# ScalarE instead of SyncE begins the stores of the expert output rows

## The reference, cut to what matters

```python
ids = g_top[:, None] * EXPERTS_PER_GROUP + e_idx          # two experts for each token
gates = jnp.einsum('nk,nke->ne', g_w * e_w, jax.nn.one_hot(ids, N_EXPERTS))
for e in range(N_EXPERTS):
    a = jax.nn.silu(hf @ w_e_gate[e]) * (hf @ w_e_up[e])  # 1024 -> 512, twice
    out = out + gates[:, e:e + 1] * (a @ w_e_down[e])     # 512 -> 1024
```

## Time and profile before

| | |
|---|---|
| runs | 1700.65, 1700.78, 1700.83 us |
| profiled execution | span 1698.5 us from first to last instruction; with the 2.3 us around it, the 1700.8 us of the runs |
| TensorE, VectorE, ScalarE busy | 1633.7, 1331.4, 1035.4 us |
| experts | about 340 to 912 us |
| stores of expert rows | 35 on SyncE's queue: 10 of 512 KB, 8 of 256 KB, 17 of 128 KB |

### The profile page before, as it was taken

The page is one execution under the profiler, slowest core; times in us unless marked ns, Lnnn a source line. Parts: engine busy times, 40 slices in busy tenths (PEclk is TensorE's granted clock), DMA queues, the critical chain, the costliest instruction groups (busy, mean ns, idle before and its releaser), DMA issues.

```text
span 1698.5 us, 27843 instructions
## 1 busy us (share of the span) xinstructions
PE 1633.7 (96%) x10558; PEld 1427.5 (84%) x10558; DVE 1331.4 (78%) x1522; ACT 1035.4 (61%) x1145; POOL 64.0 (4%) x58
## 2 busy tenths in 40 slices
PE   8999989999999999999998998999999999999998
PEld 7998879878877677777776987999999999998887
DVE  6546897874589999999996897778767979777776
ACT  4333676554678999999987554554444484453443
POOL 0000000000000000000003340000000020000000
PEclk9999999999999999999999999999999999999999
DMA  9663126085789999999999443446555455445550
GB/s 327 191 191 103 54 72 202 9 322 184 269 342 422 422 422 423 422 423 423 423 420 338 144 164 105 149 149 202 195 176 171 152 191 185 144 141 194 195 175 25
DMA packets 186669, 393.26 MB, mean 232 GB/s; under 512 B 6992, under 2 KB 151120, under 8 KB 162000
## 3 DMA queue, kind: packets, MB, share of 16 engines
q1 hardware_dynamic: 184496, 383.89, 61.8%
q0 software_dynamic: 2080, 8.10, 1.3%
HBM read 381.34 MB, written 10.62 MB: 231 GB/s over the span
## 4 chain that ended last, share of the span: by engine, by line
PE 58%; DMA 16%; DVE 14%; issue 6%; ACT 5%; SPq 0%; POOL 0%; DVEq 0%; ACTq 0%; POOLq 0%
DMA raw<-w_e_up_dram 13%; PE ps L979 9%; DVE wlo L2377 7%; PE ps L693 5%; PE ps L698 5%; PE ps L985 5%; PE ps L694 5%; PE ps L994 4%; PE ps L1165 3%; PE ps L1120 2%; PE ps L1114 2%; PE ps L1116 2%; ACT whi L1680 2%; PE ps L1036 1%; PE ps L1044 1%
## 5 line engine op out<-in xcount | busy, mean ns | idle before, releaser
L2377 DVE TENSOR_TENSOR wlo<-raw,whi 128x2048 fp32r<-128x2048 f32 (+2 forms) x358 | 811.6, 2279 | 167.4 <-ACT whi L1680 159.6
L1680 ACT ACTIVATE whi<-raw 128x2048 fp32r<-128x2048 f32 (+2 forms) x358 | 675.7, 1891 | 302.0 <-PE ps L985 113.8
L693 PE MATMUL ps<-xh,whi 128*128 128x256 f32 x672 | 166.2, 287 | 3.2 <-DVE xl L2390 2.0
L694 PE MATMUL ps<-xl,whi 128*128 128x256 f32 x672 | 163.9, 284 | 0.0
L1114 PE MATMUL ps<-whi,xh 128*128 128x512 f32 x528 | 160.3, 396 | 0.6 <-ACT whi L1680 0.6
L979 PE MATMUL ps<-xb,whi 128*128 128x512 f32 x672 | 160.2, 390 | 0.0
L1120 PE MATMUL ps<-wlo,xh 128*128 128x512 f32 x528 | 143.7, 396 | 3.2 <-DVE wlo L2377 3.2
L979 PEld LDWEIGHTS ps<-xb,whi 128*128 128x128 f32 x672 | 124.0, 188 | 24.4
L693 PEld LDWEIGHTS ps<-xh,whi 128*128 128x128 f32 x672 | 129.5, 193 | 4.3 <-issue 1.8
L694 PEld LDWEIGHTS ps<-xl,whi 128*128 128x128 f32 x672 | 129.4, 193 | 0.2
L1120 PEld LDWEIGHTS ps<-wlo,xh 128*128 128x128 f32 x528 | 97.0, 188 | 32.8 <-DVE wlo L2377 13.1
(11 more groups left out here) (502 smaller groups left out, 3082.2 us busy)
## 6 DMA issues: line engine op xcount, KB each, us to landing
raw<-w_e_gate_dram SPq DMA_DIRECT2D x64, 1024.0 KB, 10.6
raw<-w_e_up_dram SPq DMA_DIRECT2D x64, 1024.0 KB, 10.7
raw<-w_e_down_dram SPq DMA_DIRECT2D x64, 1024.0 KB, 10.5
raw<-ffn_w_gate_up_dram SPq DMA_DIRECT2D x44, 1024.0 KB, 5.1
raw<-w_in_dram SPq DMA_DIRECT2D x30, 1024.0 KB, 5.6
raw<-ffn_w_down_dram SPq DMA_DIRECT2D x22, 1024.0 KB, 4.9
raw<-xa_w_kv_dram SPq DMA_DIRECT2D x16, 1024.0 KB, 5.5
raw<-xa_w_q_dram SPq DMA_DIRECT2D x8, 1024.0 KB, 5.3
```

Source lines behind the costliest of these rows:

```text
L693: nc.tensor.matmul(o[b], wh, h, start=b == 0 and a == 0, stop=False, skip_group_check=True)
L694: nc.tensor.matmul(o[b], wh, l, start=False, stop=False, skip_group_check=True)
L1680: nc.scalar.activation(whi[u % HL][:, 0:n], raw[u % RAW][:, 0:n], ACT.Copy).then_inc(hi_ready, 1)
L2377: v.tensor_tensor(wlo[u % HL][:, 0:n], raw[u % RAW][:, 0:n], whi[u % HL][:, 0:n].bitcast(F32), ALU.subtract).then_inc(lo_ready, 1)
```

## The change

`store` and its row numbers move from SyncE's program to ScalarE's `y_there`. A row number is now loaded ahead of the eviction, and the store is begun directly behind it: wait until the eviction is done, wait until the store before has landed, issue. A tile with two passes evicts both first, and then begins both stores. The stores of tile m - 2 are now in tile m, where those of m - 3 were. ScalarE's loop is split at tile 17, since the row count of a store is fixed in the code.

```diff
 # SyncE
-            def store(s, n, i=None):
-                add = 0 if i is None else i * LOOP
-                row = row_start(s, i)
-                sp.wait_ge(r_y, add + s + 1)
-                sp.sem_inc(store_go, 1)
-                if i is not None or s >= 1:
-                    sp.wait_ge(y_stored, (0 if i is None else i * (16 * LOOP)) + 16 * s)
-                    sp.sem_inc(store_go, 1)
-                sp.dma_start(compact[bass.ds(row, n), :], y_out[s % 2][0:n, :]).then_inc(y_stored, 16)
...
                     load(u + 4, wdn[0][before], i=i, step=s)
-                    for a in passes(m - 3) if m >= 3 else ():
-                        store(a, rows_of(m - 3), i)
                     load(u + 5, wdn[1][before], i=i, step=s)
...
-            late_stores = {moe + 6 * TILES: passes(TILES - 3),
-                           moe + 6 * TILES + 3: (*passes(TILES - 2), *passes(TILES - 1))}
...
                     load(u, units[u][0])
-                    for a in late_stores.get(u, ()):
-                        store(a, last_rows)
 # ScalarE
+                def store(s, n, row, i=None):
+                    act.wait_ge(r_y, (0 if i is None else i * LOOP) + s + 1)
+                    act.sem_inc(store_go, 1)
+                    if i is not None or s >= 1:
+                        act.wait_ge(y_stored, (0 if i is None else i * (16 * LOOP)) + 16 * s)
+                        act.sem_inc(store_go, 1)
+                    act.dma_start(compact[bass.ds(row, n), :], y_out[s % 2][0:n, :]).then_inc(y_stored, 16)
...
+                def y_there(u, m, i=None, few=False):
+                    row = [row_start(s, i) for s in passes(m)]
                     act.wait_ge(unit_used, (0 if i is None else i * (6 * LOOP)) + u)
                     first, w = passes(m)[0], P if m < HEAVY else SLOTS
                     for s in passes(m):
...
                         nc.scalar.activation(y_out[s % 2][0:w, :], ps[0:w, at:at + 2, :].rearrange("p b n -> p (b n)"),
                                              ACT.Copy).then_inc(r_y, 1)
+                    for s, r in zip(passes(m), row):
+                        store(s, rows_of(m), r, i)
```

More of the change, by code:

```diff
@@ L610, in tile @@
                     load(u + 4, wdn[0][before], i=i, step=s)
-                    for a in passes(m - 3) if m >= 3 else ():
-                        store(a, rows_of(m - 3), i)
                     load(u + 5, wdn[1][before], i=i, step=s)
-                for m in range(1, HEAVY + 3):
+                for m in range(1, HEAVY + 1):
                     tile(m)
[L617 to L622, removed]
+                with sp.Fori(0, (TILES - HEAVY - 1) // LOOP) as i:
+                    for m in range(HEAVY + 1, HEAVY + 1 + LOOP):
+                        tile(m, i)
+                for m in range(HEAVY + 1 + (TILES - HEAVY - 1) // LOOP * LOOP, TILES):
                     tile(m)
@@ L626, in load_experts @@
                     load(p0 + 6 * TILES - 2 + a, wdn[a][e])
-            late_stores = {moe + 6 * TILES: passes(TILES - 3),
-                           moe + 6 * TILES + 3: (*passes(TILES - 2), *passes(TILES - 1))}
-            last_rows = rows_of(TILES - 1)
             def ffn_cols(l, half):
@@ L1859, in silu_turned, with rows_of @@
                     nc.scalar.activation(sil[s % 2][:, 0:256], ps[:, 6, 0:256], ACT.Silu).then_inc(r_silu, 1)
-                def y_there(u, m, i=None):
+                def rows_of(m):
+                    return P if m < HEAVY else SLOTS if m < FEW else SLOTS // 2
+                def store(s, n, row, i=None):
[7 more added lines that the diff above has]
+                    row = [row_start(s, i) for s in passes(m)]
                     act.wait_ge(unit_used, (0 if i is None else i * (6 * LOOP)) + u)
@@ L1952, in experts @@
                     tile(m)
[L1953 to L1957, removed]
+                for first, end in ((HEAVY + 2, FEW + 2), (FEW + 2, TILES - 1)):
+                    assert (end - first) % LOOP == 0
+                    with act.Fori(0, (end - first) // LOOP) as i:
+                        for m in range(first, first + LOOP):
+                            tile(m, i)
+                tile(TILES - 1)
                 u = p0 + 6 * TILES
```

## The result

The changed kernel takes 1717.24 us, the median of four runs (1716.11 to 1718.88), against 1700.72 for the kernel before: a ratio of 1.0099, 95% interval 1.0086 to 1.0113. It is 16.5 us slower. The forecast was 1695.5 us, with 1691 to 1707 as its range: the sign and the range were both wrong.

The account below looks back on a forecast made before the run. TensorE is busy 1633.7 of 1698.5 us; weight loads pace the light tiles. The terms -2 + 0 + 1.1 - 4.4 = -5.3 us against 1700.78 gave 1695.5 us, range 1691 to 1707.

Parts of the forecast that it names:

- Part 3: Light tiles: the store costs ScalarE 1.0 to 1.1 us a tile against 1.1 us idle, row load hidden: 0 us.
- Rival C: Light tiles: store above 1.35 us makes ScalarE the bound; 1703 us, or 1725 with a 2.07 us issue; chance 0.15.
- Its sign, a DMA share under 1: In the light tiles of the new profile, a DMA share under 1 would show ScalarE as the bound.
- Part 2: Two-pass tiles: ScalarE stalls 3.5 to 5 us for landings; TensorE +5.1, less 2.5, about +2.7 us up to tile 5.
- Both together, -2 us: Start of the DMA-bound stretch: TensorE's 2.7 us lag leaves the load queue full, loads go out on time; -4 to +2.8.
- Part 1: Before the light tiles: SyncE's stalls go; 2.5 of a 3.40 us ScalarE wait counted for TensorE, 2.8 us idle DMA time usable.
- Part 4: End of the experts: tile 31's silu +1.1 us late, earlier gathers close TensorE's holes of 2.90 and 1.54 us, -4.4 us.
- Rival B: Stores on ScalarE's queue don't pass the loads; tile 31's takes 7.97 us: +5, 1706 us; chance 0.10.

Follow-up runs that it names:

- light_behind_hi: Changed kernel with the store in light tiles of 64 rows begun behind the next hi copy, not directly behind the eviction: 1706.63 us, ratio 1.0042.
- all_behind_hi: Changed kernel with each store begun behind one or two hi copies in all tiles, except tile 31's store: 1695.57 us, ratio 0.9969 to the kernel before.
- the two best kernels: all_behind_hi at 1695.57 us, and the same kernel with the stores of tiles 30 and 31 begun by SyncE: 1694.31 us.
- tail_only: Kernel before with only the stores of tiles 29 to 31 begun by ScalarE, directly behind their evictions: 1702.25 us, ratio 1.0009.
- tail_behind_hi: Kernel before with stores of tiles 29 to 31 on ScalarE, those of 29 and 30 behind the next hi: 1698.85 us, ratio 0.999.
- stop_long: Kernel before, all stores on SyncE; ScalarE in each light tile waits for its eviction, then loads two row numbers: 1717.22 us, ratio 1.0092.

## Why the prediction was wrong

**Part 3 is the step that failed.** "Laid end to end a tile takes ScalarE about 13.9 us, and 15.0 with the store, under the 15.2 of the loads", so "0 us". The store was sized well (0.91 us of 1.0 to 1.1), the row load is hidden, and the loads still have a share of 1.01. But ScalarE's idle time was taken as slack. ScalarE is one arc of a ring whose other arcs, VectorE's `wlo` and TensorE's unit, take the rest of the tile. The `hi` can't run earlier, since `unit_used` gives it its buffer only when TensorE has been through, so the idle time ahead of it could not be spent. The ring's slack was 0.39 us, not 1.1 to 1.35. "VectorE and TensorE are late by some 1 us in every tile, but by the same amount in each" holds for a delay that nothing feeds back; here it comes round through `unit_used`. That is 10.6 us (light_behind_hi).

Rival C, ScalarE as the bound for a price above 1.35 us, had the right side and the wrong mechanism: the issue was no dearer (0.33 us), and ScalarE was busy 322.43 of 364.97 us. Its sign, a DMA share under 1, did not come either, though the loads had slowed down. The rows of before already posed the question: with 1.1 us idle on ScalarE and 0.3 on TensorE no engine is full, so how far one may be late is a question to the ring, and nowhere did the prediction add one up.

**Part 2 was right in its mechanism and too small, by a factor of 1.7 to 2.** Stalls of 3.5 to 5 us were forecast, "more where loads are in flight", and 2.90, 3.98 and 6.68 measured (4.76 for the last in light_behind_hi). TensorE was to lose 2.0 and 3.1 us, 5.1 in all. Against all_behind_hi, and with the 1.55 us that the profiles differ by at tile 0 taken off, tile 2's eviction is 3.8 us later (468.08 against 462.76) and tile 3's 10.6 us later (491.91 against 479.80): 3.8 and 6.8, part of it from the late end of one store and the slower matmuls behind the wait. The same reading of light_behind_hi gives 3.8 and 4.9 (466.26 and 488.18, 0.34 taken off the other way).

**"Both together, -2 us" fell with it.** Its lower end, -4 with the stalls hidden, is passed by all_behind_hi: tile 5 at 519.86 instead of 522.42, tile 13 at 642.97 instead of 647.90, tile 28 at 871.67 instead of 877.43. But with the stalls the lag of the changed kernel behind the kernel before was 7.1 us at tile 3 (491.91 against 483.08, less 1.8), and not the 2.7 of the sum (its terms, 5.1 less 2.5, make 2.6). Of -2 us nothing came, and 8.3 us were lost up to tile 5. That such a lag empties the queue is my reading. Part 1, the end of SyncE's stalls, is the likely source of the 4.5 to 7 us by which the two best kernels beat the kernel before, since in all_behind_hi 5.8 us are gained at tile 28; no run takes SyncE's stalls away by themselves. The share of 0.66 at 245 GB/s from 340 to 484 us (before 0.70 at 259) shows that loads were lost there.

**Part 4: -3.3 forecast, +0.1 measured** (from the eviction of tile 30 to the end of the span 796.2 us before and 796.3 after; the end moved alone: +1.4). The silu is 0.73 us late instead of 1.1 (TensorE waits 2.15 us for 1.42). The store of tile 31 was to take 3 us and took 4.96, and the gathers were to be quicker beside the loads and were not: 7.8 us for the four, before 7.6. From the last eviction to the first gather it is 7.13 us, before 8.05. The gain is 0.9 us and the silu takes most of it.

**Rival B did not happen.** In the changed kernel a store of 128 KB lands in 5.6 us on ScalarE's queue, where it took 9.2 on SyncE's. But its loads also land sooner there (7.0 to 7.5 us instead of 10.5), so this is not yet the same load. all_behind_hi is: its loads flow at 422 GB/s as before, and land in 10.5 us. From 640 to 880 us, before the change and in all_behind_hi:

```profile
raw<-w_e_down_dram SPq DMA_DIRECT2D x30, 1024.0 KB, 10.5
compact_y<-arena SPq DMA_DIRECT2D x13, 128.0 KB, 9.2
```

```profile
raw<-w_e_up_dram SPq DMA_DIRECT2D x31, 1024.0 KB, 10.5
compact_y<-arena ACTq DMA_DIRECT2D x14, 128.0 KB, 5.2
```

So a second queue passes queued loads, but in part only. By the Trainium skill (DMA: Bandwidth & Descriptors, "Issuing engines are not separate DMA queues") all of them share the DMA engines and interleave, and only the time to begin a DMA is saved. The trace agrees with the first in that a store still takes 5 us beside loads and 2.0 on idle engines. It doesn't agree with the second: 4.0 us of landing are saved.

## What to carry to other kernels

An engine's idle time is not its slack. Where buffers go round between three engines, add up one turn of the ring, stop included, and compare that with the pace of the loads; only the difference can be spent, and a small stop, put in by hand, measures it. And a DMA issue that waits for something belongs behind the instruction that others wait for: moved behind the next `hi` or two, the same stores turned a loss of 1% into a gain of 0.3%, because a queue that waits holds everything behind it, on ScalarE as on SyncE.

## What was not expected of the hardware

After a wait of 4.66 us TensorE ran eight matmuls at 0.43 us each instead of 0.23, half of full speed, the lower of its clocks (1.2 for 2.4 GHz); the granted clock was 0.61 from 478 to 482 us. At the end of the experts, where it waits for tile 31's silu, the length of the wait did not tell what followed. After 2.15 us it ran the same way for some 6 us in tail_only (granted clock 0.58 over 8 us), and not at all in the changed kernel. After 1.43 us it ran so in all_behind_hi (0.79 over 8 us), and not in tail_behind_hi (1.00).

A store of 512 KB took 6.6 us to land, though from 473 to 476 us the DMA engines had a share of 0.04 to 0.06. One late part of it held ScalarE, VectorE and TensorE.

A DMA share of 1.00 or 1.01 stood beside 405 GB/s (stop_long, 530 to 880 us), 410 and 423 GB/s. A full share does not tell a queue that is kept back from one that sets the pace; the rate and the waits do.
